# Half of the weights' low parts computed by GpSimd: two of the four ring slots, with one semaphore per slot

## The reference, cut to what matters

```python
# first block
proj = rmsnorm(h) @ w_in                       # q, k, v of two mixers, gates
ya = sliding_window_attention(...) @ w_proj_a
ob = gated_linear_attention(...)               # normed, times silu(gate)
merged = sigmoid(gate_a) * ya + sigmoid(gate_b) * (ob @ w_proj_b)
h = h + merged @ w_out
h = h + (silu(z @ w_ffn_gate) * (z @ w_ffn_up)) @ w_ffn_down
x = rmsnorm(h)
# second block
proj = rms_norm(x) @ w_in_2
o_conv = (conv_y * silu(conv_z)) @ w_conv_out
o_mla  = (mla_attention(...) * silu(mla_z)) @ w_mla_out     # 16 heads
o_mem  = (memory_attention(...) * silu(mem_z)) @ w_mem_out
merged = sigmoid(g_conv) * o_conv + sigmoid(g_mla) * o_mla + sigmoid(g_mem) * o_mem
x = x + merged @ w_o
```

## Time and profile before

| what | value |
|---|---|
| median of three runs | 2991.47 us (2989.81 to 2995.59) |
| span of the profiled execution, first to last instruction | 2990.0 us |
| mean granted TensorE clock | 0.944 of full speed |
| TensorE busy (matmul) | 90% |
| VectorE busy | 64% |
| ScalarE busy | 38% |
| GpSimd busy | 0% |
| read from HBM | 459.6 MB |

### The profile page before, as it was taken

One profiled execution on the slowest core, in us unless ns is written; L12 is line 12 of the kernel. 1 busy time (PEld: TensorE's weight loads), 2 busy tenths in 40 slices (PEclk: granted clock), 3 DMA queues, 4 the chain that ended last, 5 costly groups with the idle time before them and its releaser, 6 DMA issues.

```text
span 2990.0 us, 32688 instructions
## 1 busy us (share of the span) xinstructions
PE 2682.2 (90%) x11795; PEld 2182.2 (73%) x11795; DVE 1902.8 (64%) x2501; ACT 1132.7 (38%) x1330; POOL 0.2 (0%) x4
## 2 busy tenths in 40 slices
PE   5998778999899999999987989799988988989998
PEld 4777556887688888878865767688877766767777
DVE  5555656775576677655566567556657787776654
ACT  3332333443344444434434334233433333333332
POOL 0000000000000000000000000000000000000000
PEclk9998889999899999999988999899978999989999
DMA  5843323565465665645543545366624443435543
GB/s 181 232 137 113 95 92 122 180 197 163 127 189 181 199 187 176 203 164 193 192 174 113 157 137 158 112 190 183 190 89 137 134 128 120 143 131 148 181 159 132
DMA packets 234462, 466.52 MB, mean 156 GB/s; under 512 B 19003, under 2 KB 27473, under 8 KB 233442
## 3 DMA queue, kind: packets, MB, share of 16 engines
q1 hardware_dynamic: 230496, 457.89, 48.3%
q10 hardware_dynamic: 3842, 7.01, 1.2%
HBM read 459.60 MB, written 5.24 MB: 155 GB/s over the span
## 4 chain that ended last, share of the span: by engine, by line
PE 75%; DVE 16%; issue 3%; ACT 3%; DMA 1%; DVEq 0%; SPq 0%; ACTq 0%
PE acc L430 21%; PE acc L431 21%; PE acc L432 21%; DVE arena L1477 3%; DVE w_lo L1243 3%; PE banks L489 2%; DMA raw<-in_w_in_dram 1%; DVE etmp L1472 1%; PE acc L671 1%; PE acc L673 1%; PE acc L672 1%; PE banks L671 1%; PE banks L673 1%; PE banks L672 1%; ACT w_hi L930 1%
## 5 line engine op out<-in xcount | busy, mean ns | idle before, releaser
L1243 DVE TENSOR_TENSOR w_lo<-raw,w_hi 128x1024 fp32r<-128x1024 f32 (+2 forms) x866 | 1037.6, 1218 | 796.9 <-ACT w_hi L930 776.1
L930 ACT ACTIVATE w_hi<-raw 128x1024 fp32r<-128x1024 f32 (+2 forms) x866 | 906.0, 1053 | 1423.9 <-PE acc L432 1272.1
L430 PE MATMUL acc<-w_hi,x_hi_A 128*128 128x512 f32 (+2 forms) x1824 | 741.1, 406 | 51.3 <-DVE w_lo L1243 39.1
L431 PE MATMUL acc<-w_lo,x_hi_A 128*128 128x512 f32 (+2 forms) x1824 | 724.6, 397 | 0.0
L432 PE MATMUL acc<-w_hi,x_lo_A 128*128 128x512 f32 (+2 forms) x1824 | 723.6, 397 | 0.0
L430 PE MATMUL acc<-w_hi,x_hi_B 128*128 128x512 f32 (+1 forms) x1344 | 531.7, 396 | 28.8 <-DVE w_lo L1243 15.7
L431 PE MATMUL acc<-w_lo,x_hi_B 128*128 128x512 f32 (+1 forms) x1344 | 526.2, 392 | 0.0
L432 PE MATMUL acc<-w_hi,x_lo_B 128*128 128x512 f32 (+1 forms) x1344 | 525.8, 391 | 0.0
L430 PEld LDWEIGHTS acc<-w_hi,x_hi_A 128*128 128x128 f32 x1824 | 361.6, 198 | 140.1 <-DVE w_lo L1243 43.2
L432 PEld LDWEIGHTS acc<-w_hi,x_lo_A 128*128 128x128 f32 x1824 | 359.1, 197 | 74.7
L431 PEld LDWEIGHTS acc<-w_lo,x_hi_A 128*128 128x128 f32 x1824 | 360.6, 198 | 70.0 <-issue 0.7
(11 more groups left out here) (226 smaller groups left out, 1528.9 us busy)
## 6 DMA issues: line engine op xcount, KB each, us to landing
raw<-in_w_in_dram SPq DMA_DIRECT2D x377, 512.0 KB, 4.1
raw<-in_w_ffn_gate_dram SPq DMA_DIRECT2D x88, 512.0 KB, 3.9
raw<-in_w_ffn_up_dram SPq DMA_DIRECT2D x88, 512.0 KB, 4.2
raw<-in_w_ffn_down_dram SPq DMA_DIRECT2D x88, 512.0 KB, 4.6
raw<-in_w_out_dram SPq DMA_DIRECT2D x32, 512.0 KB, 4.3
raw<-in_w_mem_kv_dram SPq DMA_DIRECT2D x32, 512.0 KB, 3.7
raw<-in_w_mla_out_dram SPq DMA_DIRECT2D x32, 512.0 KB, 4.2
raw<-in_w_o_dram SPq DMA_DIRECT2D x32, 512.0 KB, 4.2
```

Of the source, the lines that this page charges most:

```text
L430: mm(o, xh, hi[:, k, :], start=(kt == 0), stop=False)
L431: mm(o, xh, lo[:, k, :], start=False, stop=False)
L930: act.activation(w_hi[:, s, 0:n], raw[:, r, 0:n], ACT.Copy).then_inc(hi_done, 1)
L1243: dve.tensor_tensor(w_lo[:, s, 0:n], raw[:, r, 0:n], w_hi32[:, s, 0:n], ALU.subtract).then_inc(lo_done, 1)
```

## The change

GpSimd gets a queue of its own with the subtractions of slots 1 and 3, in the order of the granules; VectorE keeps those of slots 0 and 2 at their old places in its queue and only counts the others. Since two engines now finish low parts, in an order that is no longer fixed, the one counter `lo_done` becomes one per slot. TensorE waits for the count of the granule's slot, and SyncE, before it refills `raw`, for the count of the same slot. The constants of the loops stay (each loop advances the granules by a multiple of four).

```diff
+POOL_SLOTS = (1, 3)
...
-        hi_done, lo_done = sem("hi_done"), sem("lo_done")
+        hi_done = sem("hi_done")
+        lo_done = [sem(f"lo_done{i}") for i in range(SPL)]
...
-                    need(sp, lo_done, G.at(1 - RAW))
+                    need(sp, lo_done[G.slot(SPL)], G.rounds(SPL, SPL - RAW))
...
-                pe.wait_ge(lo_done, G.at(1))
                 s = G.slot(SPL)
+                pe.wait_ge(lo_done[s], G.rounds(SPL) + 1)
...
+        @block.gpsimd
+        def _(pool):
+            G = Count()
+
+            def low(n):
+                s, r = G.slot(SPL), G.slot(RAW)
+                if s in POOL_SLOTS:
+                    pool.wait_ge(hi_done, G.at(1))
+                    pool.tensor_tensor(w_lo[:, s, 0:n], raw[:, r, 0:n], w_hi32[:, s, 0:n], ALU.subtract).then_inc(lo_done[s], 1)
+                G.n += 1
+
+            def body(chunks):
+                for c in chunks:
+                    if c.name == "ffn_down":
+                        for _ in range(8):
+                            low(GRAN)
+                    else:
+                        for _ in range(c.grans):
+                            low(c.per * c.w)
+
+            for name, n, chunks in SEG:
+                if n <= 2:
+                    for _ in range(n):
+                        body(chunks)
+                else:
+                    per = 8 if name == "ffn_down" else sum(c.grans for c in chunks)
+                    with engine_loop(pool, n, {G: per}):
+                        body(chunks)
...
             def split(n):
                 s, r = W.G.slot(SPL), W.G.slot(RAW)
-                dve.wait_ge(hi_done, W.G.at(1))
-                dve.tensor_tensor(w_lo[:, s, 0:n], raw[:, r, 0:n], w_hi32[:, s, 0:n], ALU.subtract).then_inc(lo_done, 1)
+                if s not in POOL_SLOTS:
+                    dve.wait_ge(hi_done, W.G.at(1))
+                    dve.tensor_tensor(w_lo[:, s, 0:n], raw[:, r, 0:n], w_hi32[:, s, 0:n], ALU.subtract).then_inc(lo_done[s], 1)
                 W.G.n += 1
```

## The result

The change makes the kernel slower: 3041.06 us, median of four runs (3036.24 to 3041.48), against 2990.83 us for four runs of the kernel before beside them. The ratio is 1.0162 with a 95% interval of [1.0149, 1.0176]: 50 us. The profiled execution has a span of 3039.7 us at a mean granted clock of 0.935, against 2990.0 us at 0.944. The forecast was 3005 us, the upper end of its range 3020.

What follows compares the result with a forecast made beforehand. TensorE bounds the full stretches, roughly half the kernel; elsewhere its pauses, mainly in MLA, where the chain goes through VectorE. Span 2990.0 + 15 + 3.6 - 5 = 3003.6, said as 3005 us; own range 2992 to 3020, overall 2950 to 3020.

Steps and rivals of the forecast that it cites:

- Step (4): MLA stage: VectorE and GpSimd wait for each other at SBUF, two meetings a call at 2.1 us; +15 us over eight calls.
- Step (6): Outside MLA: earlier low parts at some pauses -7 us, ffn_down's start and one more place or meeting +2; net -5 us.
- step (5): MLA: a TensorE pause grown by 1.9 us brings slow-clock matmuls in two calls of eight; +3.6 us.
- Steps (1), (2): Whole kernel: VectorE loses 433 of 866 subtractions of 1.22 us; GpSimd does them at 2.45 us each.
- Step (3): One MLA call: the 4.87 us pause stays, norms begin 2.3 us earlier, GpSimd takes its granules at once.
- The first rival: Whole kernel: GpSimd and VectorE do not hinder each other, so removed subtractions are gained; 2966 us, chance 33%.
- the lines that the forecast named as signs: VectorE's scalings and subtractions (lines 1469, 2175, 2182, 1243) would take longer than 1.22 us if VectorE is held.
- Step (7): Semaphores and waits cost nothing; SyncE's refill has 8 x 2.72 us of cover against 1.2 us of delay.
- The second: MLA: meetings fall beside the path, one a call, cancelling the gain; with -5 us outside, 2987 us, chance 18%.
- The third: Full stretches: GpSimd above 5.44 us a subtraction sets the pace; at 6.55 us the kernel takes 3320 us, chance 3%.

Runs made afterwards that it cites:

- pool_writes: Changed kernel, but GpSimd subtracts one column and fills the other 1023 of its slots with zeros: 2952.00 us, 0.9867 of the kernel before.
- pool_writes_long: Changed kernel, but GpSimd does six one-column subtractions, then the zero fill, about 2.4 us planned per granule: 2961.61 us, 0.9899 of the kernel before.

## Why the prediction was wrong in its size

The sign, the mechanism and the first steps held; the sum was 36 us short (3005 for 3041), and its range ended 21 us below the result. The step that failed is the count of meetings. Step (4) took two for each call of MLA, 16 at 2.1 us; the trace has 24. Step (6) took at most one outside MLA; the trace has 92, 160 us of holding, of which the full stretches hide a part. With the clock of step (5) the MLA term was +18.6 us and is +31 to +36; the term outside MLA was -5 us and is +18.

- **Steps (1), (2)** held: 433 subtractions each; GpSimd 2.46 us for the 2.45 taken.
- **Step (3)** held where it can be checked. The long pause of each call stayed, the norms begin 2.3 us earlier, and GpSimd takes its granules during the rotary products and just at the next low parts.
- **Step (4), the choice "on which the forecast hangs"**, was right in kind and in unit price: 2.1 us a meeting forecast, 2.15 and 2.14 measured at two of them (the mean of all 116 is 1.76, so the forecast price was not too low). The first rival (nothing held) fell: VectorE's instructions did grow, and the two runs of the same relief with hardly any holding are 79 us and more below the change. The number of meetings failed: the forecast had two a call, among the scalings, rotary products and stage copies. The displayed call has three up to the sigmoid's addition (+1.27), of which no step spoke (line 1469 stood only among the signs), and a fourth in the low parts made ahead at its end; the four long calls have four each, the short ones two. Of the lines that the forecast named as signs, 1469, 2182 and 1243 grew and 2175 did not. The term +15 for eight calls is, with the clock, +31 in the trace and +36 in the run of MLA alone.
- **Step (5), the clock**, failed: slow matmuls after the new pause were expected in two calls of eight, 3.6 us in all. The displayed call, in which the forecast had TensorE "keep its clock" unless the pause grew, loses 1.4 us; the granted clock of the MLA stretch fell from 0.92 to 0.90. In MLA TensorE's busy time grew by 9 us for the 3.6 forecast. Over the whole span 0.944 became 0.935, and its busy time grew by 13 us: wide matmuls that follow each other at 0.38 to 0.48 us are 326 instead of 252. The other 36 us are pauses.
- **Step (6), outside MLA**, failed most: -5 forecast, +18 measured in the run without MLA. The gains named do exist: at the pause of 1604 us the kernel after wins 2.6 us. But the same holding as in step (4), which the forecast priced only in MLA, meets VectorE in every other mixed stage: in the gated linear attention VectorE's own low parts have 2046 ns (405 to 525 us, 11 of them), and between 308 and 552 us the kernel falls back by 10.5 us. The start of ffn_down was rightly given as a loss: 6.3 us of waiting for 5.5.
- **Step (7)** held: the semaphores are free (0.9999), and the full stretches keep their rate and so their transfers (with slots 0 and 2 they do not, as the run above shows).
- **The rivals.** The second (meetings beside the path) describes the full stretches and the first 300 us, not MLA. The third (GpSimd too slow) fell: 2.46 us are under its 5.44, and the full stretches kept their rate.
- **The range** ended at 3020 because the upper end of the price was bounded, but not the number of meetings. The rows of the prediction could have warned of that: GpSimd's 433 x 2.45 us are 1061 us, and VectorE is busy for 64% of the span before, so meetings were to be expected in every stage.

## What to carry to other kernels

When an engine gives elementwise work on SBUF tiles to GpSimd, count the relief and then every instruction of VectorE with two SBUF inputs, or of the fast SBUF-to-SBUF form, that can fall under it: each can cost nearly the whole GpSimd instruction (up to 2.2 of 2.4 us here, 1.76 on average), in all stages and not only in the one that is to be helped. It reaches the kernel's time only where VectorE's queue is on the path. Look for it in the mean durations by line, since no wait of VectorE shows it. In this kernel a low part made late cost little where its maker started as soon as the input was there (+10 to +15 us for 433 granules) and very much where it stood behind VectorE's queue (+117 us).

## What was not expected of the hardware

- A fill of 1023 columns by GpSimd (0.95 us) leaves VectorE's subtractions at 1.22 us but holds its fast copies. In pool_writes the staging copies have 810 ns instead of 427:

```profile
L1277 DVE TENSOR_TENSOR w_lo<-raw,w_hi 128x1024 fp32r<-128x1024 f32 x424 | 518.2, 1225 | 1115.8 <-ACT w_hi L932 1107.6 <-DVE arena L1637 0.3 <-DVE x_lo_B L1368 0.2
...
L1859 DVE COPY stage<-work 128x512 f32<-128x512 f32 x22 | 17.8, 810 | 0.8
...
L1244 POOL MEMSET w_lo<- 128x1023 f32 (+1 forms) x433 | 411.3, 950 | 0.0
```

  In pool_writes_long nearly the same fill comes about 1 us later, misses them, and they have 429. In pool_writes 36 of VectorE's subtractions ran beside a fill, and none was longer by more than 0.03 us. The section of the Trainium skill named above says that a VectorE instruction with two SBUF inputs contends only with a GpSimd instruction that reads SBUF; these rows agree.
- It works in both directions: GpSimd's own subtractions have a median of 2.40 us and a longest of 4.42, and 57 of the 433 take more than 2.6. The Trainium skill, GPSIMD Engine Reference, section Performance versus the Vector engine, gives 4497 ns for 2048 columns; half of it is an estimate of 2.25 us, and the 2.34 to 2.40 us of the displayed call lie 4 to 7% above it.
- Which slots GpSimd takes, and so which instructions of VectorE its subtractions meet, decides more than 10 us: slots 0 and 2 lost 63 us, 1 and 3 lost 50, 3 alone 37, and in all three the longest single holding is 2.2 us. Why slots 0 and 2 lost as much as 44 us ahead of MLA was followed only for ffn_up.
